# Two state-space/attention mixers in float32: three more projection chunks in three passes, late convolutions moved, and a square root argument rewritten

## The reference, cut to what matters

```
for l in range(2):
    proj = h @ w_in[l]
    rg_x, rg_gate, z, xbc, dt_raw, q, k, v = split(proj)
    y_a = gelu(rg_gate) * rg_lru(causal_dwconv(rg_x), ...)
    y_b = mamba2_group(z, xbc, dt_raw, ...)      # silu(causal_dwconv(xbc)), then the chunked scan
    y_c = sliding_window_attention(q, k, v, sinks)
    h = layer_norm(ALPHA * h + concat(y_a, y_b, y_c) @ w_out[l])
    h = layer_norm(ALPHA * h + peer_ffn(h, ...))

# in rg_lru
log_a = -8 * r * softplus(-lam);  a = exp(log_a)
u = sqrt(-expm1(2 * log_a)) * (i * x)
```

## Time and profile before

| | us |
|---|---|
| median of 3 runs | 3102.31 |
| lowest and highest of them | 3090.55, 3103.15 |
| profiled execution | 3098.36 |
| span in its profile | 3096.5 |
| TensorE busy in the span | 2986.0 (96%) |
| VectorE busy | 2340.3 (76%) |
| ScalarE busy | 1518.6 (49%) |

### The profile page before, as it was taken

How to read it: one execution, slowest core, us unless ns; L and a number is a source line. 1 busy time by engine, 2 the same in 40 slices (tenths; PEclk the granted TensorE clock), 3 DMA queues, 4 the chain that set the end, 5 groups by cost and what they waited for, 6 DMA issues and landing times.

```text
span 3096.5 us, 51319 instructions
## 1 busy us (share of the span) xinstructions
PE 2986.0 (96%) x16392; PEld 2525.9 (82%) x16392; DVE 2340.3 (76%) x5168; ACT 1518.6 (49%) x2658; POOL 297.1 (10%) x413
## 2 busy tenths in 40 slices
PE   7999999989999999999999999999999999999999
PEld 4888887869887879888888888777798888888887
DVE  5888888456656766997777777677679977777776
ACT  3222223245744655186555554446552855555544
POOL 0000000000000005083000000000051920000000
PEclk9999999999999999999999999999999999999999
DMA  6333332224132334413555555523354135555553
GB/s 273 118 119 110 119 125 109 82 72 150 69 109 95 110 136 150 150 56 110 188 190 190 187 185 210 190 96 112 134 164 136 55 136 186 185 186 188 190 193 133
DMA packets 75129, 440.82 MB, mean 142 GB/s; under 512 B 6976, under 2 KB 7360, under 8 KB 35200
## 3 DMA queue, kind: packets, MB, share of 16 engines
q1 hardware_dynamic: 72336, 420.23, 37.8%
q0 software_dynamic: 2672, 19.01, 1.7%
HBM read 438.16 MB, written 1.05 MB: 142 GB/s over the span
## 4 chain that ended last, share of the span: by engine, by line
PE 85%; DVE 8%; DVEq 2%; issue 2%; ACT 2%; ACTq 0%; DMA 0%; POOL 0%; SPq 0%
PE bank L477 18%; PE bank L479 17%; PE bank L478 17%; PE bank L2365 10%; PE bank L2367 5%; PE bank L2295 4%; PE bank L1534 2%; DVE arena L2568 2%; PE bank L2327 1%; PE bank L893 1%; PE bank L882 1%; PE bank L1251 1%; PE bank L1269 1%; PE bank L564 1%; DVE arena L1586 1%
## 5 line engine op out<-in xcount | busy, mean ns | idle before, releaser
L456 ACT ACTIVATE peer_r<-wring 128x512 fp32r<-128x512 f32 x1312 | 816.5, 631 | 801.8 <-PE bank L479 546.2
L461 DVE TENSOR_TENSOR peer_r<-wring,peer_r 128x512 fp32r<-128x512 f32 x1248 | 845.9, 692 | 381.9 <-ACT peer_r L456 378.5
L2365 PE MATMUL bank<-res_r,peer_r 128*128 128x512 f32 x1280 | 457.1, 397 | 3.4 <-DVE peer_r L461 3.4
L477 PE MATMUL bank<-h_r,peer_r 128*128 128x512 f32 (+1 forms) x1088 | 398.1, 366 | 22.7 <-DVE h_r L672 15.3
L477 PE MATMUL bank<-peer_r 128*128 128x512 f32 x1024 | 404.2, 395 | 2.8 <-DVE peer_r L2599 2.8
L479 PE MATMUL bank<-peer_r 128*128 128x512 f32 x1024 | 401.2, 392 | 0.0
L478 PE MATMUL bank<-peer_r 128*128 128x512 f32 x1024 | 399.5, 390 | 0.0
L479 PE MATMUL bank<-h_r,peer_r 128*128 128x512 f32 (+1 forms) x1088 | 385.6, 354 | 0.0
L2367 PE MATMUL bank<-res_r,peer_r 128*128 128x256 f32 x1280 | 359.0, 280 | 0.0
L478 PE MATMUL bank<-h_r,peer_r 128*128 128x512 f32 (+1 forms) x960 | 334.8, 349 | 0.0
L2365 PEld LDWEIGHTS bank<-res_r,peer_r 128*128 128x128 f32 x1280 | 240.5, 188 | 61.4 <-DVE peer_r L461 4.0
(11 more groups left out here) (398 smaller groups left out, 5061.8 us busy)
## 6 DMA issues: line engine op xcount, KB each, us to landing
wring<-in_w_peer SPq DMA_DIRECT2D x256, 1024.0 KB, 4.8
wring<-in_w_proj SPq DMA_DIRECT2D x34, 1024.0 KB, 4.8
wring<-in_w_hy SPq DMA_DIRECT2D x32, 1024.0 KB, 4.8
arena<-in_w_ada POOLq DMA_DIRECT2D x16, 1024.0 KB, 5.1
wring<-in_w_out SPq DMA_DIRECT2D x16, 1024.0 KB, 4.8
wring<-in_w_ada SPq DMA_DIRECT2D x8, 1024.0 KB, 11.2
wring<-in_w_hyout SPq DMA_DIRECT2D x8, 1024.0 KB, 4.8
wring<-in_w_q SPq DMA_DIRECT2D x8, 1024.0 KB, 4.8
```

Source lines behind the costliest of these rows:

```text
L456: act.activation(SPLIT[:, buf, 0, :], raw_quarter(name, i, j, q), ACT.Copy).then_inc(split_hi, 1)
L461: v.tensor_tensor(SPLIT[:, buf, 1, :], raw_quarter(name, i, j, q), SPLIT[:, buf, 0, :].bitcast(F32), ALU.subtract).then_inc(split_lo, 1)
L477: pe.matmul(out_ap, w_hi, x_hi, start=start, stop=False, **kw)
L2365: pe.matmul(two_parts(acc[:, :]), SPLIT[:, buf, 0, w], h_both[:, k, :, :], start=(k == 0), stop=False, skip_group_check=True)
```

## The change

- SPLIT_FROM is replaced by a list: chunks 3, 4 and 10 are multiplied in three passes too. Their copies and remainders are put into the lists of ScalarE and VectorE at places of their own.
- rows_scalar and rows_vector move to the start of the mixer, in the order in which the normalised activations come ready (ROWS_ORDER), with a drain and waits on h_tok.
- 1 - a*a is computed as th*(1 + a*a): ScalarE squares a (RG 3 into RG 5) behind the tanh, VectorE does one operation; addition and reciprocal go.
- In VectorE's list conv_vector 4 moves from behind inputs 0 to behind the first remainder of chunk 11, and conv_vector 5 is cut into its two tiles, which go among the remainders of chunk 12 and behind those of chunk 13. In ScalarE's list silu 4 and silu 5 move with them.
- In the arena PT3, VTK, ST get places of their own, SM goes to its start (over SQ), MH_LO to the second half of res, YQ over RG.

```diff
-SPLIT_FROM = 11
+SPLIT_CHUNKS = (3, 4, *range(10, 17))
...
-        MH_LO = view(arena_r("mh_lo", RG_AT, KT * T)[:, :], KT)
+        PT3 = c3.take(2, 3 * P)
+        VTK = c3.take(2, P)
+        ST = [c3.take(8, 8) for n in range(2)]
+        YQ = Carve(RG_AT).take(KT, T)
...
-        cw = Carve(BLOCKS * T)
+        cw = Carve()
         SM = [cw.take(2, 2 * T) for n in range(2)]
...
-        YQ = tmp
+        MH_LO = h_hi
...
-            if j == SPLIT_FROM:
+            if j == SPLIT_CHUNKS[0]:
                 pe.wait_ge(mh_lo, 4 * (l + 1))
...
+        ROWS_ORDER = (1, 3, 0, 2)
+
         def rows_scalar(act, l):
-            for k2 in range(4):
+            act.drain()
+            for n, k2 in enumerate(ROWS_ORDER):
+                if n >= 2:
+                    act.wait_ge(h_tok, 4 * l + n + 1)
                 act.activation(two_tiles(MH_HI, k2), two_tiles(h, k2), ACT.Copy).then_inc(mh_hi, 1)
...
-            proj_chunk(pe, l, 3)
+            proj_split(pe, l, 3)
             values_tensor(pe, l)
-            proj_chunk(pe, l, 4)
+            proj_split(pe, l, 4)
...
-                (proj_split if t else proj_chunk)(pe, l, 10 + t)
+                proj_split(pe, l, 10 + t)
...
                 act.activation(RG[:, 4, t * T:(t + 1) * T], r, ACT.Tanh, scale=MU[:, 4 + t:5 + t])
-            act.drain().then_inc(a_ready, 1)
+                if t == 2:
+                    proj_hi(act, l, 4, (0,))
+            act.drain()
+            act.activation(RG[:, 5, :], RG[:, 3, :], ACT.Square).then_inc(a_ready, 1)
...
         def mixer_scalar(act, l):
+            rows_scalar(act, l)
             decay_scalar(act, l)
-            for j in range(3):
+            for j in range(2):
                 proj_out(act, l, j)
+            proj_hi(act, l, 3, range(4))
+            proj_out(act, l, 2)
             gates_scalar(act, l)
+            proj_hi(act, l, 4, (1, 2))
             proj_out(act, l, 3)
+            proj_hi(act, l, 4, (3,))
             values_scalar(act, l)
             root_scalar(act, l)
...
             proj_out(act, l, 8)
-            rows_scalar(act, l)
             turned_scalar(act, l, 3)
+            proj_hi(act, l, 10, range(4))
             silu_scalar(act, l, 3)
             proj_out(act, l, 9)
             segment_scalar(act, l, 0)
+            state_scalar(act, l, 0)
+            proj_hi(act, l, 11, range(3))
+            proj_out(act, l, 10)
+            proj_hi(act, l, 11, (3,))
+            segment_scalar(act, l, 1)
             silu_scalar(act, l, 4)
-            state_scalar(act, l, 0)
-            act.wait_ge(sw_pv, 4 * l + 4)
-            proj_hi(act, l, 11, range(4))
-            proj_out(act, l, 10)
-            segment_scalar(act, l, 1)
-            silu_scalar(act, l, 5)
             state_scalar(act, l, 1)
...
             z_scalar(act, l, 0)
+            silu_scalar(act, l, 5)
...
             th, u = RG[:, 4, :], RG[:, 5, :]
-            v.tensor_scalar(u, th, 1.0, None, ALU.add)
-            v.drain()
-            v.reciprocal(u, u)
-            v.drain()
-            v.scalar_tensor_tensor(u, th, 2.0, u, ALU.mult, ALU.mult).then_inc(root_in, 1)
+            v.scalar_tensor_tensor(u, u, 1.0, th, ALU.add, ALU.mult).then_inc(root_in, 1)
...
-        def conv_vector(v, l, k):
+        def conv_vector(v, l, k, tiles=(0, 1)):
...
-            for e in range(2):
+            for e in tiles:
...
-            a.then_inc(x_conv, 1)
+            if 1 in tiles:
+                a.then_inc(x_conv, 1)
...
         def mixer_vector(v, l):
+            rows_vector(v, l)
             softplus_rows(v, l)
             gates_vector(v, l)
+            proj_lo(v, l, 3, range(4))
+            proj_lo(v, l, 4, (0,))
             root_vector(v, l)
+            proj_lo(v, l, 4, (1, 2, 3))
             columns_vector(v, l)
...
             window_out(v, l, 2)
-            rows_vector(v, l)
             cb_vector(v, l, 0)
             inputs_vector(v, l, 0)
-            conv_vector(v, l, 4)
+            proj_lo(v, l, 10, range(4))
             window_out(v, l, 3)
             v.drain().then_inc(mix_ready, 1)
             decayed_vector(v, l, 0)
             inputs_vector(v, l, 1)
-            conv_vector(v, l, 5)
-            proj_lo(v, l, 11, range(4))
+            proj_lo(v, l, 11, (0,))
+            conv_vector(v, l, 4)
+            proj_lo(v, l, 11, (1, 2, 3))
             sum_vector(v, l, 0)
             decayed_vector(v, l, 1)
             inputs_vector(v, l, 2)
-            proj_lo(v, l, 12, range(3))
+            proj_lo(v, l, 12, (0, 1))
+            conv_vector(v, l, 5, (0,))
+            proj_lo(v, l, 12, (2,))
             sum_vector(v, l, 1)
...
             proj_lo(v, l, 13, range(3))
+            conv_vector(v, l, 5, (1,))
             sum_vector(v, l, 2)
```

More of the change, by code:

```diff
@@ L259, in program @@
         TSD, TNM = stats[:, 28:30], stats[:, 30:32]
-        cw = Carve(BLOCKS * T)
+        cw = Carve()
         SM = [cw.take(2, 2 * T) for n in range(2)]
[L263 to L266, removed]
+        assert cw.at <= KT * T
         G = arena[:, 0:BLOCKS * T].rearrange("p (j t) -> p j t", j=BLOCKS)
@@ L435, in stream_pairs @@
                              src[first + RING * i + j]).then_inc(w_landed[s], 16)
-        split_chunks = lambda name, n: {"proj": 17 - SPLIT_FROM, "pre": PRE_SPLIT}.get(name[:-1], n)
+        split_chunks = lambda name, n: {"proj": len(SPLIT_CHUNKS), "pre": PRE_SPLIT}.get(name[:-1], n)
         SPLIT_PHASES = [(name, split_chunks(name, n)) for name, n, _ in PHASES if name != "ada" and name[:3] != "mid"]
@@ L1538, in proj_unit @@
         def proj_unit(l, j, q):
-            return unit_of(f"proj{l}", 0, UNITS * (j - SPLIT_FROM) + q)
+            return unit_of(f"proj{l}", 0, UNITS * SPLIT_CHUNKS.index(j) + q)
         def proj_split(pe, l, j):
@@ L1560, in proj_lo @@
                 lo_quarter(v, f"proj{l}", 0, j, q, proj_unit(l, j, q), q, q == UNITS - 1)
+        ROWS_ORDER = (1, 3, 0, 2)
         def rows_scalar(act, l):
-            for k2 in range(4):
+            act.drain()
+            for n, k2 in enumerate(ROWS_ORDER):
+                if n >= 2:
+                    act.wait_ge(h_tok, 4 * l + n + 1)
                 act.activation(two_tiles(MH_HI, k2), two_tiles(h, k2), ACT.Copy).then_inc(mh_hi, 1)
         def rows_vector(v, l):
-            for k2 in range(4):
-                v.wait_ge(mh_hi, 4 * l + k2 + 1)
+            for n, k2 in enumerate(ROWS_ORDER):
+                v.wait_ge(mh_hi, 4 * l + n + 1)
                 v.tensor_tensor(two_tiles(MH_LO, k2), two_tiles(h, k2), two_tiles(MH_HI, k2).bitcast(F32),
@@ L1573, in proj_out @@
             b, _ = bank_of(f"proj{l}", 0, j)
-            if j < SPLIT_FROM:
+            if j not in SPLIT_CHUNKS:
                 wait_done(act, f"proj{l}", 0, j)
```

## The result

The kernel after takes 3082.44 us (median of 4 runs, 3078.9 to 3084.84), the kernel before 3101.55 (4 runs, 3090.55 to 3103.15): a ratio of 0.9943, with a 95% interval of 0.9928 to 0.9958; the two medians alone are 19.1 us apart. The profiled execution of after took 3082.02 us, 16.3 less than that of before. The forecast was 3082 and a gain of 16.7. The size fits; the profile shows that it came about in another way than forecast.

The account below looks back on a forecast made before the run. TensorE, 85% of the chain, was taken as the bound, with VectorE neck and neck in chunks 5 to 9. Layer gains of 9.1 and 7.75 less 0.1 made 16.7 us: 3098.4 to 3081.7, given as 3082, range 3070 to 3096.

Parts of the forecast that it names:

- chunk 9 earlier: Rounds up to chunk 9: VectorE's lead from the cheaper root starts chunk 9 2.2 us earlier per layer.
- chunks 10 and 11, their wait: Chunk 10 saves 1.17 us, chunk 11 its 3.13 us wait, plus slow clock of 2.60 (layer 0) or 1.25 (layer 1).
- late convolutions, rest: Moved convolution 5 and silu around chunks 12 and 13: taken as zero cost, up to 1 us a layer.
- parts of the activations: Copies and subtractions moved to the mixer's front: cost taken as 0.1 us, bounded by 0.5 us in layer 1.
- Chunk 4's wait: Inside chunk 4, TensorE waits 1.95 us for remainders 1 to 3, which stand behind root_vector's second operation.
- rival A: The 1.95 us wait in chunk 4 drops the clock; gain 13.3 us, 3085 us; chance 0.12.
- Rival B: VectorE late at chunk 11, TensorE stands for convolution 4's rest; 4 us less gain, 3086 us; chance 0.12.
- the lead: From convolution 0 on, VectorE runs 2.2 us ahead per layer, up to chunk 9.
- the root's part: VectorE's root needs one 1.23 us operation instead of 0.69 + 6.55 + 1.23; root_in at 973.2 instead of 979.0.
- C: Rival: VectorE late by a convolution at chunks 4, 10 and 11; slower than before, 3114 us; chance 0.07.
- Rival D: Rounds don't shorten, another wait holds chunk 9; gain 12.3 us, 3086 us; chance 0.14.
- The square: ScalarE's square behind the tanh, 1.06 us for 1024 columns, with no table load added.

Follow-up runs that it names:

- rem1_early: The kernel after with remainder 1 of chunk 4 put between root_vector's two operations; 3081.39 us, 0.9952 of before.
- root_only: The kernel before with only 1-a*a rewritten (square on ScalarE, one operation on VectorE); 3094.87 us, 0.9992 of before.
- late_convs_only: The kernel before with only convolutions 4 and 5 moved back and activations' parts at the front; 0.9974 of before.
- chunk4_plain: The kernel after with chunk 4 alone left as a plain float32 chunk; 3076.05 us, 0.9938 of before.
- reciprocal_back: The kernel after with the old root_vector (addition, reciprocal, product; no square); 3092.6 us, 0.9988 of before.
- before_again: The kernel before, unchanged, run again for a second profile; timed once, 3092.09 us.
- chunk4_plain_2: The kernel after with chunk 4 alone left plain, run again on another chip for a second profile; 3075.56 us, 0.9939 of before.
- after_again: The kernel after, unchanged, run again for a second profile; 3082.12 us, 0.9955 of before.
- seg0_early: The kernel after with segment_scalar of tile 0 ahead of chunk 9's eviction on ScalarE; 3080.93 us, 0.9954 of before.
- plain4_seg0: The kernel after with chunk 4 plain and segment_scalar of tile 0 ahead of chunk 9's eviction; 3074.31 us, 0.9931 of before.

## Why the prediction was right, and where it was not

**The time was right, one step was wrong, and that the total fitted so closely was luck.** By terms, in us, over both layers (the ledger's columns up to chunk 9, then from there to chunk 11's end, then the rest):

```
                                  forecast        measured
chunk 9 earlier                   2.2  + 2.2      0.82 + 0.43
chunks 10 and 11, their wait
and the clock behind it           6.9  + 5.55     6.97 + 5.62
late convolutions, rest           0    + 0        0    + 0
parts of the activations         -0.1             0 (layer 1)
sum                               16.7            13.85
```

The measured column takes the first profile of each kernel. By their ledger the 13.85 us are 10.25 at chunk 11 (wait and slow clock), 4.2 by the rounds between scores and chunk 9, 2.3 by chunk 3 and 2.3 by chunk 10, less 5.2 lost in chunk 4.

**Chunk 4's wait: the length held, the clock did not.** I had forecast 1.95 us; it was 2.05 and 2.04, because the remainders came just where they were placed (first ready 975.05, forecast 975.1). But I let the clock stay at 1.00, on the 2.23 us wait at the start of the kernel, behind which it did, and gave rival A 0.12. In all four mixers of after it fell, to 0.51 to 0.57 over the 2 us behind the wait. The chunk ended at 981.08, not 979.45, 1.6 us late in layer 0. Of this 0.15 is a slip in my sum: a start at 975.15 and three quarters of 5.93 us end at 979.6. The clock took 1.2 by rem1_early, 1.3 by the rows (14 distances of 0.213 us instead of 0.119, up to 978.48) and 1.5 in layer 1 (16 of them). The step that failed is "with the clock at 1.00" behind that wait, and so the term of 2.2 a layer. Rival A's own time, a gain of 13.3, is what the mixers show against the mean of both profiles of before. The row that I leaned on, a wait of nearly the same length, stood among other work, and was no bound for this one. Rival B leaned on it as well (stands under 2.3 us leave the clock alone), and that is wrong for the same reason.

**The rest of the lead.** Scores to chunk 9 took 41.55 and 41.92 us, 2.28 and 1.91 less than before, so the root's part was sized well, as root_only shows with 1.94 and 2.29. It shows as 0.82 and 0.43 at chunk 9 only because chunks 3 and 4 together are 1.46 and 1.48 us longer than they were (1.15 less in chunk 3, 2.6 more in chunk 4). Convolution 0 started at 990.00, not at the forecast 988.3, held as said by chunk 5's eviction, which came later with the chunk: what chunk 4 loses goes through to chunk 9 in full.

**Chunks 10 and 11.** Here each step held. VectorE's timeline in after, the remainders 1 to 3 of chunk 11 and 2 of chunk 12:

```profile
1041.12 1.89 DVE L461 TENSOR_TENSOR peer_r<-wring,peer_r 128x512 fp32r<-128x512 f32 x3
1049.63 0.69 DVE L461 TENSOR_TENSOR peer_r<-wring,peer_r 128x512 fp32r<-128x512 f32 x1
```

Chunk 10 takes 5.93 us; remainder 1 of chunk 11 was ready at 1041.8 and wanted at 1043.8, a slack of 2.0 us (forecast 2.2); remainder 2 of chunk 12 ready at 1050.3, wanted at 1053.6 (forecast 1048.8 and 1052.1). The forecast had a slip here too: chunk 10 was to start at 1032.7, not 1032.5 (1034.27, 0.67 of broadcasts, less the 2.2), and the slack would then have read 2.4. late_convs_only shows that the order of VectorE's work ahead of chunk 11 is what removed the wait and its slow stretch. Rival B, a stand behind convolution 4, did not come; nor did C. Rival D named a wait that holds chunk 9; root_only argues against it, since the rounds did shorten.

**The square.** No table load stood before it in any profile: it takes 1.06 us, behind tanh, and as forecast costs no more. The page ScalarE: Activation LUTs of the Trainium skill (The consequence) charges a load for a switch to another named set, but doesn't say to which sets square belongs. The traces show that none is loaded for it here.

**The activations' parts at the front** cost nothing: from dt to the transposes layer 1 takes 28.95 us in before and 28.94 in chunk4_plain and in reciprocal_back, which both have them there. In the other executions it took 30.6 to 31.2, with the parts at the front or without (before_again 30.87, root_only 31.13). In layer 0 it is the same picture: 28.93 in before_again and in chunk4_plain_2, 30.3 to 30.5 in the others. The windows of the first 5 us behind dt, in chunk4_plain and in before_again, show what differs:

```profile
2002.41:2007.41 5.00, 5.00 (x23) 2.76 (x24) 3.88 (x9) 3.72 (x6) 0.00 (x0) 1.00 0.00 0
```

```profile
2008.76:2013.76 5.00, 5.00 (x15) 1.91 (x16) 0.00 (x0) 1.25 (x1) 0.00 (x0) 0.61 0.00 0
```

The granted clock was 1.00 in the one and 0.61 in the other. That is about 2 us of chance in a stretch that lies ahead of the ledger's mixer, and part of the spread outside.

**Why 16.7 still fitted.** Against a sum that was 2.9 us too high (3.4 against the mean of both profiles of before) stood 2.35 us outside the mixers, which are chance. So the close fit of the profiled execution (3082.02 against 3082) is luck. A forecast by 13.3 would have said 3085, inside the range as well. What can be told from the timed runs alone is a gain of 0.30 to 0.72% (by both comparisons), 9 to 22 us, which holds 16.7 and 13.3 alike; the split into terms rests on the ledger. The mean of the four runs of before that I gave as 3098.5 is 3098.6, which changes nothing.

## What to carry to other kernels

Before a chunk is made shorter at the price of a wait on another engine, put the wait's whole price beside the saving, the slow clock behind it included: chunk 4 in three passes saves 1.17 us of TensorE and cost 2.6 net. Most of the gain came from ordering VectorE's queue so that what TensorE wants next does not stand behind a lump of 4 us. And where runs of one kernel spread over 4 to 14 us, a ledger of fixed points in the trace tells effects of 1 us, which the medians cannot; compare it over two profiles of the same kernel first.

## What the runs showed of the hardware

Waits of 2.03 to 2.06 us in the middle of chunk 4 lowered the granted clock in six of six mixers (after, after_again, seg0_early), and the waits of 8.34 us in reciprocal_back did in both, while one of 2.23 us at the kernel's start did not the earlier trace rows. The clock also fell inside chunk 10, behind the 1.19 us wait for the exponentials, in layer 0 of rem1_early, chunk4_plain and root_only, for 1.5 to 1.7 us, and not in layer 1 of these, nor in after or chunk4_plain_2 with the same wait: in 3 of the 20 mixers that have it. So the length of the wait alone doesn't decide, and a short one that a profile shows as harmless may cost in the next execution. That seg0_early and plain4_seg0 take away the wait ahead of chunk 10, and had 1.00 there in four of four mixers, agrees with this, but is too few to show it. The wait ahead of chunk 11 in before cost between 1.2 and 2.6 us in slow clock beside its own 3.13. VectorE's reciprocal over 128x1024 took 6.55 us, where the product of the same size took 1.23.
